# Output projection of a two-layer hybrid trunk: one float32 product becomes three float32r products, with split weights kept in DRAM and one buffer for their high halves

## The chip, the cores and the metric

The kernel runs on one core of a Trainium2 chip. The metric is the device time of one execution in microseconds (us), the median over several executions. The engines are TensorE (PE; its weight loads are shown as PEld), VectorE (DVE), ScalarE (ACT), GpSimd (POOL) and SyncE (SP), which here only issues DMAs.

## The reference

Two layers over x of 1024 rows and 1024 columns, float32. A layer normalises x, multiplies by `w_in` and sends column groups through three mixers (gated DeltaNet with 4 heads, a state space model with 16 heads in 2 groups, retention with 4 heads). Their outputs are normalised, gated and concatenated to `mixed`, 2048 wide. The change is about the last lines:

```python
o_a = rmsnorm(o_a, gdn_norm) * silu(gz)             # 512 columns
o_b = rmsnorm(y_b per group, ssd_norm per group)     # 2 x 512 columns
o_c = rmsnorm(o_c, ret_norm) * silu(rg)             # 512 columns
mixed = concatenate([o_a, o_b, o_c])
out = mixed @ w_out                                 # 2048 x 1024
x = x + rmsnorm(out, post_norm)
```

The weight of each of these norms belongs to a row of `w_out`, so it can be applied to `mixed` or to the rows of `w_out`.

## The kernel before, in words

**Parts.** The work is done in 4 parts: layer 0 rows 0 to 511 (part 0), layer 0 rows 512 to 1023 (part 1), then the same for layer 1 (parts 2, 3). A part of 512 rows is 4 tiles of 128 (`NT`). The float32 product of the input projection is already done as three float32r products: each operand is split in a high part (rounded to float32r) and a low part (the rest), and high x high, low x high and high x low are added. In an even part the weights are split as they arrive (`split`: ACT copies to `w_hi`, POOL subtracts to `w_low`) and both parts are stored to `w_split` in DRAM (`keep`); the odd part after it, of the same layer, loads both from there.

**Input projection.** `w_in` comes in 26 pieces of 256 columns (`PIECES`; two are in SBUF, `W_RING`). A piece is 16 planned `proj` steps, called slices here. The wide pieces use 128x512 matmuls, the narrow ones (gates and retention) 128x256: stationary `hT`, moving `w`, 6 matmuls a slice.

**Output projection.** `mixed` has 4 groups of 512 columns: DeltaNet, two of the state space model, retention. When a group of a part is ready, `mix_turn` transposes its 4 tiles on PE and DVE multiplies each 128x512 bank by the norm weights into `mixT`. Then come its output steps, `("out", p, group, unit, tp)`: the 1024 output columns are 4 units of 256 columns (`UNITS`), and `tp` is a pair of tiles, so 8 steps a group, 32 a part. A unit is 512 KB of `w_out` (128 partitions x 4 row blocks x 256), loaded by SP (line 996) into one of two buffers of `wo_loaded` and used by two steps. A step has 2 x 4 float32 matmuls of 128x256; the trace records each of them as two. DVE adds the bank to `acc` (lines 1572, 1575). After the last unit of group 3 come `squares` and `final` (norm, residual, store).

**Order.** `make_plan` writes out one order of steps for all engines: each engine goes through `plan` and does its share. The planner keeps a clock for each engine, a due time for each result, and picks in this order: side work that is due, a `mix_turn` if no output step is left open, the next mixing step if due within `NEAR` ns, else an output step, if it is due and (the front is late, or stuck, or the next mixing step is more than `OUT_WAIT` away and `APART` slices have gone since the last output step), else the next front step. The front is stuck where `frees` names a buffer still in use: gate pieces 12 and 13 wait for `mix_turn` of group 3 of the part before, 16 and 17 for that of group 0, the retention pieces (from 18 on) for that of group 1, the first piece of the next part for that of group 2. SP's DMAs are one list, `loads`, sorted by the place in the plan that frees their buffer; SP waits for each in turn (line 978: for the stores of `w_split` before a piece buffer is overwritten).

## Time and profile before

| | |
|---|---|
| median of 3 runs | 2396.87 us (2395.07 to 2397.87) |
| the profiled execution | 2396.32 us, its span 2394.5 us |
| granted TensorE clock, mean | 0.996 of full speed |
| busy PE / DVE / ACT / POOL | 2313.7 / 1303.8 / 761.9 / 503.8 us |
| DMA | 339.27 MB, 142 GB/s on the mean |

The span runs from the first to the last instruction. A matmul's duration includes its way through the array, so neighbouring matmuls overlap; the distance between their starts is what one costs. "idle before" is the time an engine stood ahead of an instruction, and behind the arrow is what ended it.

### The profile page before, as it was taken

Reading aid. Unit: us, or ns where it says so; the run is one execution under the profiler, and the core shown is the slowest. Engines: PE = TensorE matmul, PEld = TensorE weight load, DVE = VectorE, ACT = ScalarE, POOL = GpSimd, SP = SyncE. Lnnn points to the kernel's source line nnn. Section 1 sums busy time; section 2 is a strip of 40 time slices with the busy share of each in tenths; the row PEclk is TensorE's granted clock in tenths of the full one; section 3 lists DMA queues with packets and bytes.
Section 4 is the critical chain, followed back from the end, with each engine's and each line's share of the span. In section 5 each row is a group of like instructions: output and inputs, shape, how many; then the busy total and the mean of one; then the engine's idle time right before and its main releaser. Section 6 shows DMA issues by size and latency. Waiting matters only on the chain. (4 is left out here: it accounts for less than half of the span.)

```text
span 2394.5 us, 37085 instructions
## 1 busy us (share of the span) xinstructions
PE 2313.7 (97%) x15032; PEld 2044.7 (85%) x15032; DVE 1303.8 (54%) x2284; ACT 761.9 (32%) x1373; POOL 503.8 (21%) x448
## 2 busy tenths in 40 slices
PE   5999999999999999999999999999999999999995
PEld 4887888998888889899888898889988889889995
DVE  3766578435556565624555756853445554573233
ACT  3644344232423234112444423422233323331000
POOL 2443333330100011101243323423211000110000
PEclk9999999999999999999999999999999999999998
DMA  5644422555323324343544442545632232343412
GB/s 190 230 159 158 159 106 97 190 207 195 122 86 100 116 88 151 131 144 123 203 173 167 167 154 93 184 142 197 237 130 93 93 115 80 129 153 98 158 54 97
DMA packets 78649, 339.27 MB, mean 142 GB/s; under 512 B 8976, under 2 KB 9744, under 8 KB 65040
## 3 DMA queue, kind: packets, MB, share of 16 engines
q1 hardware_dynamic: 77760, 335.45, 41.0%
q8 instruction: 121, 1.98, 0.3%
q10 hardware_dynamic: 720, 1.45, 0.2%
q14 instruction: 48, 0.39, 0.0%
HBM read 219.42 MB, written 117.44 MB: 141 GB/s over the span
## 5 line engine op out<-in xcount | busy, mean ns | idle before, releaser
L1024 PE MATMUL ps<-w_hi,hT_hi 128*128 128x256 f32 x1792 | 526.2, 294 | 1.6 <-POOL w_low L1958 1.6
L1024 PE MATMUL ps<-w_low,hT_hi 128*128 128x256 f32 x1792 | 504.6, 282 | 0.0
L1024 PE MATMUL ps<-w_hi,hT_lo 128*128 128x256 f32 x1792 | 499.8, 279 | 0.0
L1024 PE MATMUL ps<-wo_loaded,mixT 128*128 128x256 f32 x2048 | 457.7, 379 | 3.5 <-DVE et L1592 3.4
L1024 PEld LDWEIGHTS ps<-wo_loaded,mixT 128*128 128x128 f32 x2048 | 384.0, 190 | 60.1 <-issue 5.8
L1958 POOL TENSOR_TENSOR w_low<-w_loaded,w_hi 128x512 fp32r<-128x512 f32 x208 | 284.4, 1384 | 449.1 <-ACT w_hi L1718 449.0
L1024 PEld LDWEIGHTS ps<-wk 128*128 128x128 f32 x2336 | 294.9, 191 | 92.4 <-DVE wk L1479 30.2
L1024 PE MATMUL ps<-wk 128*128 128x128 f32 (+2 forms) x2336 | 343.3, 286 | 11.4 <-DVE wk L1502 1.8
L1024 PEld LDWEIGHTS ps<-w_low,hT_hi 128*128 128x128 f32 x1792 | 340.3, 190 | 1.3 <-issue 0.2
L1024 PEld LDWEIGHTS ps<-w_hi,hT_hi 128*128 128x128 f32 x1792 | 337.0, 188 | 3.8 <-POOL w_low L1958 2.3
L1024 PEld LDWEIGHTS ps<-w_hi,hT_lo 128*128 128x128 f32 x1792 | 339.3, 189 | 0.0
L1024 PE MATMUL ps<-hT_hi,w_hi 128*128 128x512 f32 x768 | 333.9, 435 | 1.1 <-POOL w_low L1958 1.1
L1024 PE MATMUL ps<-hT_lo,w_hi 128*128 128x512 f32 x768 | 303.0, 395 | 0.0
L1024 PE MATMUL ps<-hT_hi,w_low 128*128 128x512 f32 x768 | 301.1, 392 | 0.0
L1387 DVE SCALAR_TENSOR_TENSOR slot<-raw,par,slot 128x512 f32<-128x512 f32 x240 | 215.0, 897 | 48.4 <-ACT slot L1751 32.9
L1575 DVE TENSOR_TENSOR acc<-acc,ps 128x512 f32<-128x512 f32 x96 | 65.8, 686 | 227.7 <-PE ps L1024 227.1
L1024 PEld LDWEIGHTS ps<-hT_lo,w_hi 128*128 128x128 f32 x768 | 144.1, 188 | 35.7
L1024 PEld LDWEIGHTS ps<-hT_hi,w_hi 128*128 128x128 f32 x768 | 145.3, 189 | 22.3 <-POOL w_low L1958 2.7
L1024 PEld LDWEIGHTS ps<-hT_hi,w_low 128*128 128x128 f32 x768 | 145.6, 190 | 20.1
L1718 ACT ACTIVATE w_hi<-w_loaded 128x512 fp32r<-128x512 f32 x208 | 121.2, 621 | 98.4 <-DMA w_loaded<-in_w_in 98.4
L1918 POOL TENSOR_TENSOR rs<-rs,con 128x4 f32<-128x4 f32 x32 | 34.9, 1090 | 477.9 <-DVE rs L1317 477.9
L1489 DVE TENSOR_TENSOR wk<-ps,con 128x512 f32<-128x512 f32 x96 | 66.3, 691 | 101.6 <-PE ps L1024 101.3
(178 smaller groups left out, 2721.1 us busy)
## 6 DMA issues: line engine op xcount, KB each, us to landing
w_loaded<-in_w_in SPq DMA_DIRECT2D x104, 512.0 KB, 5.1
w_split<-w_hi SPq DMA_DIRECT2D x52, 1024.0 KB, 8.1
w_split<-w_low SPq DMA_DIRECT2D x52, 1024.0 KB, 10.1
w_hi<-w_split SPq DMA_DIRECT2D x104, 512.0 KB, 5.5
w_low<-w_split SPq DMA_DIRECT2D x104, 512.0 KB, 6.6
wo_loaded<-in_w_out SPq DMA_DIRECT2D x64, 512.0 KB, 3.6
wk<-in_x SPq DMA_DIRECT2D x8, 512.0 KB, 6.4
xfin<-in_x SPq DMA_DIRECT2D x8, 512.0 KB, 5.2
```

The lines of the kernel that those rows point to most:

```text
L1024: return nc.tensor.matmul(o, a, b, start=start, stop=stop)
L1387: stt(o, r[:, j:j + HALF], w[:, j:j + 1], o, ALU.mult, ALU.add).then_inc(S["conv_done"], 1)
L1489: empty(tt(PP, bank4(s), over_rows(mask), ALU.mult), s)
L1575: empty(tt(o, o, b, ALU.add), s)
L1718: A(w_hi[:, n % W_RING, j * 512:(j + 1) * 512], wr[:, n % W_RING, j * 512:(j + 1) * 512], ACT.Copy)\
L1918: tt(rs[:, 12:16], rs[:, 8:12], pw[:, 0:4], ALU.pow).then_inc(S["o_rstd"], 1)
L1958: tt(w_lo[at], wr[at], w_hi[at], ALU.subtract)\
```

## The change

Each operand of the output projection is split. `mix_turn`: ACT copies the transposed bank to `mixT_hi` (float32r), DVE then subtracts it from the bank into `mixT_lo`; the norm weights go to the units. In an even part a new side step `split_out` takes a raw unit: ACT writes `wo_hi` = unit x norm weight for each row block, DVE writes unit x weight - `wo_hi` into the unit's own buffer (`wo_parts`). SP stores both parts to `wo_split` (`keep_unit`). In an odd part SP loads the low part into the ring of two, as before the unit, and the high part (`high`) into `wo_hi`, of which there is one buffer: it is loaded when the last step of the unit before is done. The four units of the last group of part 3 (`TAIL` and on) are loaded, both parts, into the buffers of the projection pieces after the last projection (`tail`). An output step has 24 float32r matmuls of 128x256 in place of 8 float32 ones. Smaller edits: `rot` lies in `raw`, with a wait of ACT for `ret_sum`; the planner's constants `SPLIT_FROM`, `APART`, `NEAR` and `UNIT` change, and it knows when units are there; the scratch for dynamic DMAs goes from 1024 to 512.

```diff
+            return [("mixT", p, r[0], 2 * r[2] + 1), ("unit", out_no(step))]
+        if k == "split_out":
+            return [("raw", out_no(step))]
...
+                if n == PARTS * len(PIECES) - 1:
+                    for u in range(UNITS):
+                        at["unit", TAIL + u] = dma(MB, "n")
...
+        elif k == "split_out":
+            mark("n", act(1700, *after))
+            mark(("unit", out_no(step)), both(1700, "n"))
         elif k == "out":
             mark("n", pe(UNIT))
+            if r[2] == NT // 2 - 1:
+                u = out_no(step)
+                at["raw", u + 2] = dma(MB // 2, "n")
+                if (u + 1) // (GROUPS * UNITS) % 2 and u + 1 < TAIL:
+                    at["unit", u + 1] = dma(MB // 2, "n")
...
+        if step[0] == "out" and step[4] == NT // 2 - 1:
+            p, u = divmod(out_no(step) + 1, GROUPS * UNITS)
+            if p % 2 == 0 and p < PARTS:
+                sides["unit"].append(("split_out", p, *divmod(u, UNITS)))
...
-        unit = outs[0] if outs and ("small", smalls) in done else None
+        unit = outs[0] if outs and ("small", smalls) in done and (outs[0][1] % 2 or ("split_out", *outs[0][1:4]) in done) else None
...
-SPLIT_FROM = 6
-APART = 20
-NEAR = 150
+SPLIT_FROM = 7
+APART = 10
+NEAR = 300
 FAR = 1e12
-SLICE, LINE, TURN, UNIT, TABLE, MB = 705, 224, 109, 16 * 216, 1283, 3200
+SLICE, LINE, TURN, UNIT, TABLE, MB = 705, 224, 109, 24 * 119, 1283, 3200
+
+
+TAIL = (PARTS * GROUPS - 1) * UNITS
+
+
+def out_no(step):
+
+    return (step[1] * GROUPS + step[2]) * UNITS + step[3]
+
+
+def unit_split_no(u):
+
+    return u - GROUPS * UNITS * ((u // (GROUPS * UNITS) + 1) // 2)
...
+    wo_split = nc.dram_tensor("wo_split", (GROUPS * UNITS, 2, P, 4 * PC), F32, kind="Internal").ap()
...
-        mixT = sb("mixT", 4, HALF)
+        mixT_hi, mixT_lo = sb("mixT_hi", 4, HALF, dtype=F32R), sb("mixT_lo", 4, HALF, dtype=F32R)
+        wo_hi = sb("wo_hi", 4 * PC, dtype=F32R)
...
-        rot = sb("rot", 512)
+        rot = raw[:, 0, 0:512]
...
+            if s[0] == "split_out" or s[0] == "out" and s[1] % 2 and s[4] == 0 and out_no(s) < TAIL:
...
+            if u[0] == "out" and u[1] % 2:
+                loads.append((where[(*out_before(u), NT // 2 - 1)], n, ("high", *u[1:])))
+            elif u[0] == "out":
+                loads.append((where[(*u, 0)], n, ("keep_unit", *u[1:])))
...
+        for u in range(UNITS):
+            loads.append((where["proj", PARTS - 1, len(PIECES) - 1, 1, Q - 1], u, ("tail", PARTS - 1, u)))
...
+                elif kind == "keep_unit":
+                    k = out_no(key)
+                    sp.wait_ge(S["wo_lo_ready"], 4 * unit_split_no(k) + 4)
+                    sp.dma_start(wo_split[k % (GROUPS * UNITS), 0], wo_hi[:].bitcast(F32)).then_inc(wo_hi_kept, 16)
+                    sp.dma_start(wo_split[k % (GROUPS * UNITS), 1], wo_parts[:, n % 2, :].bitcast(F32)).then_inc(wo_kept[n % 2], 16)
+                elif kind == "high":
+                    k = out_no(key)
+                    before = out_before(key)
+                    wait_filled(sp, (*before, NT // 2 - 1))
+                    if before[1] % 2 == 0:
+                        sp.wait_ge(wo_hi_kept, 16 * (unit_split_no(k - 1) + 1))
+                    sp.dma_start(wo_hi[:].bitcast(F32), wo_split[k % (GROUPS * UNITS), 0]).then_inc(wo_hi_in, 16)
+                elif kind == "tail":
+                    for v in range(W_RING):
+                        wait_filled(sp, ("proj", PARTS - 1, len(PIECES) - 1 - v, 1))
+                    k = (GROUPS - 1) * UNITS + n
+                    hi, lo = tail_parts(n)
+                    sp.dma_start(hi.bitcast(F32), wo_split[k, 0]).then_inc(tail_in[n], 16)
+                    sp.dma_start(lo.bitcast(F32), wo_split[k, 1]).then_inc(tail_in[n], 16)
                 else:
                     if n >= 2:
                         wait_filled(sp, unit_use(units[n - 2]))
+                        if kept_units(n - 2):
+                            sp.wait_ge(wo_kept[n % 2], 16 * kept_units(n - 2))
                     if kind == "small":
                         sp.dma_start(wo[:, n % 2, 0:KD * NSM], w_small[p // 2].rearrange("p k n -> p (k n)")).then_inc(wo_in[n % 2], 16)
+                    elif p % 2 == 0:
+                        sp.dma_start(wo[:, n % 2, :], w_out[p // 2, key[2], key[3]]).then_inc(wo_in[n % 2], 16)
                     else:
-                        sp.dma_start(wo[:, n % 2, :], w_out[p // 2, key[2], key[3]]).then_inc(wo_in[n % 2], 16)
+                        k = out_no(key) % (GROUPS * UNITS)
+                        sp.dma_start(wo_parts[:, n % 2, :].bitcast(F32), wo_split[k, 1]).then_inc(wo_in[n % 2], 16)
...
+                    k_out = out_no(s)
+                    if k_out >= TAIL:
+                        hi, lo = tail_parts(u)
+                        if tp == 0:
+                            pe.wait_ge(tail_in[u], 32)
+                    else:
+                        r = unit_no[s[:4]] % 2
+                        hi, lo = wo_hi[:], wo_parts[:, r, :]
+                        if tp == 0 and p % 2:
+                            loaded_unit(pe, s[:4])
+                            pe.wait_ge(wo_hi_in, 16 * (k_out - GROUPS * UNITS * (p // 2 + 1) + 1))
+                    hi, lo = (a.rearrange("p (k n) -> p k n", k=4) for a in (hi, lo))
                     b = opened(s)
-                    if tp == 0:
-                        loaded_unit(pe, s[:4])
                     for v in range(2):
                         t = 2 * tp + v
                         wait_emptied(pe, ("mix_turn", p, G, t))
+                        o = b[:, v * PC:(v + 1) * PC]
                         for kk in range(4):
-                            i = mm(b[:, v * PC:(v + 1) * PC], mixT[:, kk, t * P:(t + 1) * P], w[:, kk, :], kk == 0, kk == 3)
+                            if p % 2 == 0 and tp == 0 and v == 0:
+                                pe.wait_ge(S["wo_lo_ready"], 4 * unit_split_no(k_out) + kk + 1)
+                            m_hi, m_lo = (m[:, kk, t * P:(t + 1) * P] for m in (mixT_hi, mixT_lo))
+                            mm(o, m_hi, hi[:, kk, :], kk == 0, False)
+                            mm(o, m_hi, lo[:, kk, :], False, False)
+                            i = mm(o, m_lo, hi[:, kk, :], False, kk == 3)
...
-                        empty(tt(mixT[:, :, t * P:(t + 1) * P], bank4(tag), over_cols(par[:, l, Q_MIX + 4 * s[2]:Q_MIX + 4 * s[2] + 4]),
-                                 ALU.mult), tag)
+                        dve.wait_ge(S["mix_hi"], NT * (GROUPS * p + s[2]) + t + 1)
+                        empty(tt(mixT_lo[:, :, t * P:(t + 1) * P], bank4(tag), mixT_hi[:, :, t * P:(t + 1) * P], ALU.subtract), tag)
+                elif k == "split_out":
+                    r = unit_no["out", *s[1:]] % 2
+                    for kk in range(4):
+                        dve.wait_ge(S["wo_hi_ready"], 4 * unit_split_no(out_no(s)) + kk + 1)
+                        at = slice(kk * PC, (kk + 1) * PC)
+                        q = Q_MIX + 4 * s[2] + kk
+                        stt(wo_parts[:, r, at], wo[:, r, at], par[:, l, q:q + 1], wo_hi[:, at], ALU.mult, ALU.subtract)\
+                            .then_inc(S["wo_lo_ready"], 1)
...
+                elif k == "mix_turn":
+                    for t in range(NT):
+                        tag = (*s, t)
+                        wait_filled(act, tag)
+                        A(mixT_hi[:, :, t * P:(t + 1) * P], bank4(tag), ACT.Copy).then_inc(S["mix_hi"], 1)
+                elif k == "split_out":
+                    u = ("out", *s[1:])
+                    k_out = out_no(s)
+                    r = unit_no[u] % 2
+                    loaded_unit(act, u)
+                    if k_out:
+                        before = out_before(u)
+                        wait_filled(act, (*before, NT // 2 - 1))
+                        if before[1] % 2 == 0:
+                            act.wait_ge(wo_hi_kept, 16 * (unit_split_no(k_out - 1) + 1))
+                    for kk in range(4):
+                        at = slice(kk * PC, (kk + 1) * PC)
+                        q = Q_MIX + 4 * s[2] + kk
+                        A(wo_hi[:, at], wo[:, r, at], ACT.Copy, scale=par[:, l, q:q + 1]).then_inc(S["wo_hi_ready"], 1)
...
+                        if m == 0 and p:
+                            act.wait_ge(S["ret_sum"], 2 * RH * p)
```

## Rows read from the trace of the kernel before

**Rows 1.** The page: busy us, share and count of engines; one group of instructions.

```profile
PE 2313.7 (97%) x15032; PEld 2044.7 (85%) x15032; DVE 1303.8 (54%) x2284; ACT 761.9 (32%) x1373; POOL 503.8 (21%) x448
...
L1024 PE MATMUL ps<-wo_loaded,mixT 128*128 128x256 f32 x2048 | 457.7, 379 | 3.5 <-DVE et L1592 3.4
```

**Rows 2.** Stretches: length, busy us and count of PE, PEld, DVE, ACT, POOL, clock, DMA, GB/s.

```profile
0.00:345.00 345.00, 305.82 (x1885) 259.27 (x1886) 202.85 (x352) 151.55 (x289) 122.08 (x103) 1.00 0.48 173
345.00:2300.00 1955.00, 1937.56 (x12789) 1722.99 (x12788) 1069.09 (x1887) 603.31 (x1072) 375.73 (x336) 1.00 0.41 139
2300.00:2370.00 70.00, 70.00 (x362) 62.42 (x360) 21.51 (x36) 4.74 (x9) 1.75 (x3) 1.00 0.22 68
2370.00:2394.50 24.50, 0.31 (x2) 0.00 (x0) 10.37 (x9) 2.33 (x5) 4.19 (x6) 0.58 0.43 150
```

**Rows 3.** PE in order of time, two narrow pieces: start us, us, what.

```profile
1019.78 0.28 PE L1024 MATMUL ps<-w_hi,hT_hi 128*128 128x256 f32 x1
...
1023.88 0.28 PE L1024 MATMUL ps<-w_hi,hT_lo 128*128 128x256 f32 x1
...
2296.08 0.28 PE L1024 MATMUL ps<-w_hi,hT_hi 128*128 128x256 f32 x1
...
2299.92 0.28 PE L1024 MATMUL ps<-w_hi,hT_lo 128*128 128x256 f32 x1
```

**Rows 4.** PE in order of time: output steps of parts 1 and 2.

```profile
976.80 7.17 PE L1024 MATMUL ps<-wo_loaded,mixT 128*128 128x256 f32 x32 [0.67 <-DVE et L1592]
...
987.43 3.62 PE L1024 MATMUL ps<-wo_loaded,mixT 128*128 128x256 f32 x16
...
994.39 13.98 PE L1024 MATMUL ps<-wo_loaded,mixT 128*128 128x256 f32 x64
...
1477.07 10.52 PE L1024 MATMUL ps<-wo_loaded,mixT 128*128 128x256 f32 x48
...
1497.46 7.17 PE L1024 MATMUL ps<-wo_loaded,mixT 128*128 128x256 f32 x32 [0.67 <-DVE et L1592]
...
2082.33 17.48 PE L1024 MATMUL ps<-wo_loaded,mixT 128*128 128x256 f32 x80
```

**Rows 5.** PE in order of time, from the last projection on.

```profile
2300.04 1.03 PE L1027 MATMUL ps<-con,slot 128*128 128x128 f32 x8
2300.91 3.62 PE L1024 MATMUL ps<-wo_loaded,mixT 128*128 128x256 f32 x16
...
2314.58 0.38 PE L1024 MATMUL ps<-st_r,wk 128*128 128x128 f32 x2
2314.80 0.61 PE L1024 MATMUL ps<-slot,wk 128*128 128x128 f32 x4
2315.25 3.62 PE L1024 MATMUL ps<-wo_loaded,mixT 128*128 128x256 f32 x16
...
2323.50 17.43 PE L1024 MATMUL ps<-wo_loaded,mixT 128*128 128x256 f32 x80
...
2342.51 27.79 PE L1024 MATMUL ps<-wo_loaded,mixT 128*128 128x256 f32 x128
```

**Rows 6.** Loads of a unit, line 996: time from issue to landing.

```profile
DMA to landing us min/median/max: 3.3/3.6/13.4
```

**Rows 7.** DMA in the 18 us from 582 to 600, where a piece is loaded.

```profile
DMA packets 720, 2.62 MB, mean 146 GB/s; under 512 B 80, under 2 KB 80, under 8 KB 720
...
q1 hardware_dynamic: 720, 2.62, 43.8%
```

**Rows 8.** Single lines: count, ns min/median/max, first and last start, shapes.

```profile
L1798 ACT ACTIVATE wk<-ps,dec x56: 345/368/369, 136.7 to 1997.6; 128x128 f32<-128x128 f32 x56
...
L1751 ACT ACTIVATE slot<-raw,par x48: 721/724/729, 60.1 to 1902.5; 128x512 f32<-128x512 f32 x48
...
L1744 ACT ACTIVATE raw<-ps x96: 576/583/594, 59.5 to 2082.6; 128x512 f32<-128x512 f32 x96
...
L1343 DVE SCALAR_TENSOR_TENSOR hT_lo<-ps,par,hT_hi x128: 340/343/352, 23.0 to 1738.6; 128x128 fp32r<-128x128 f32 x128
...
L1387 DVE SCALAR_TENSOR_TENSOR slot<-raw,par,slot x240: 734/750/1897, 64.1 to 2106.9; 128x512 f32<-128x512 f32 x120
...
L1958 POOL TENSOR_TENSOR w_low<-w_loaded,w_hi x208: 1261/1289/2262, 18.6 to 1703.6; 128x512 fp32r<-128x512 f32 x104
```

**Rows 9.** SP's own waits: us in total, times, longest.

```profile
SPq L978 <- DMA w_split<-w_low: 404.5, 48, 11.7
```

More of the change, by code:

```diff
@@ L500, in make_plan @@
     done, smalls = {("small", -1)}, -1
-    sides = {k: [] for k in ("ssd", "fin", "norm", "post", "scale", "split")}
+    sides = {k: [] for k in ("ssd", "fin", "norm", "post", "scale", "split", "unit")}
+    sides["unit"].append(("split_out", 0, 0, 0))
     turns = [("mix_turn", p, g) for p in range(PARTS) for g in range(GROUPS)]
@@ L887, in hybrid_kernel @@
                 units.append(("small", s[1]))
-            if s[0] == "out" and s[4] == 0:
-                units.append(s[:4])
+            if s[0] == "split_out" or s[0] == "out" and s[1] % 2 and s[4] == 0 and out_no(s) < TAIL:
+                units.append(("out", *s[1:4]))
         unit_no = {u: i for i, u in enumerate(units)}
+        out_before = lambda u: ("out", (out_no(u) - 1) // (GROUPS * UNITS), *divmod((out_no(u) - 1) % (GROUPS * UNITS), UNITS))
         unit_use = lambda u: u if u[0] == "small" else (*u, NT // 2 - 1)
@@ L942, in x_rows, with tail_parts, kept_units @@
             return (x if p < 2 else x1)[r:r + P, :]
+        def tail_parts(u):
+            at = (slice(None), u // 2, slice(u % 2 * 4 * PC, (u % 2 + 1) * 4 * PC))
+            return w_hi[at], w_lo[at]
+        def kept_units(n):
+            return sum(units[m][0] == "out" and units[m][1] % 2 == 0 for m in range(n % 2, n + 1, 2))
         @block.sync
@@ L1417, in _ @@
                         wait_emptied(dve, tag)
-                        tt(own, own, rot[:], ALU.add).then_inc(S["ret_sum"], 1)
+                        tt(own, own, rot, ALU.add).then_inc(S["ret_sum"], 1)
                         dve.wait_ge(S["ret_sum"], m + 1)
```

16 lines of the change are left out of this document (10 added, 6 removed).

## Prediction

> **What bounds the kernel now.** I read the table of engines first: TensorE (PE) is busy for 2313.7 of 2394.5 us, VectorE (DVE) for 1303.8, ScalarE (ACT) for 761.9 [rows 1]. Then the stretches: of PE's 80.8 us without work, 39.2 lie in the first 345 us, 17.4 in the 1955 us up to 2300, none from 2300 to 2370, and 24.2 in the rest, behind the last matmul [rows 2]. So what PE issues is the time; every us of PE work removed counts, unless a new wait takes its place. The other engines matter only as sources of such waits. The third view is PE's order of time, in which one sees how long an output step takes and which steps stand directly behind one another.
>
> **The matmuls.** There are 128 output steps (4 parts, 4 groups, 4 units, 2 pairs of tiles). The 2048 matmul records [rows 1] are 16 to a step, two for each float32 matmul. A run of 128 records takes 27.79 us with a tail of about 0.16 on the last one, so 216 ns each and 3.46 us a step [rows 5]. The new step has 24 float32r matmuls of 256 columns. The narrow projection pieces already issue this form: 36 of them start between 1019.78 and 1023.88, 117 ns apart, and 33 between 2296.08 and 2299.92, 120 ns apart [rows 3]. Weight loads are in those pitches. A step then costs 24 x 117 = 2.81 to 24 x 120 = 2.88 us. The saving is 128 x 0.65 = 83 at one end and 128 x 0.58 = 74 at the other; I take **78 us**.
>
> **One high buffer in the odd parts.** In parts 1 and 3 the high half of unit u+1 may only be loaded when PE has done unit u. SP then issues it (0.33 us) and a 512 KB load lands 3.3 to 13.4 us after issue, median 3.6 [rows 6]. With the hand-over I put a reload at 3.9 us (3.6 to 13.7). It is free when PE has a mixing step or projection slices to do in between, and exposed when units follow one another. In the order of before they do at these places: part 1 group 0 has three boundaries between units, in the stretch from 976.80 to the end of the run at 994.39; part 3 group 0 has the same three 1164 us later, part 1 group 3 has three from 1477.07 on [rows 4], part 3 groups 1 to 2 four behind the last projection [rows 5]. Between these steps PE does nothing, or 0.7 to 3.5 us of other work. Taking off that work, the 13 boundaries lack 8.2 + 8.2 + 8.2 + 12.5 = 37 us. That is the upper end if the order stays; the lower is 0, if the changed planner fills all of them. It knows the load time of a unit now, asks for 10 instead of 20 projection slices between units, and of before's 128 steps 110 lie ahead of 2300 (all but the 18 of [rows 5]), one in 18 us on the mean of the 1955 us [rows 2], so there is room for more of them ahead of the places where the front is stuck, and the bunches shrink. For the three bunches outside the end (24.6 us) I take half, 12 us.
>
> The end is worse than its four boundaries. The last projection matmul is at 2299.92 [rows 3]; behind it came 18 output steps: two of group 1, eight of group 2 (the last five in one run), eight of group 3 [rows 5]. With the closer spacing about 12 remain: two units of group 2 and the four of group 3. At the same moment SP issues the tail, 8 x 512 KB, into the buffers of the projection pieces, and the next high reload stands behind it on the same queue. 2.62 MB took a 43.8% share of 18 us, so 332 GB/s while it ran [rows 7]; 4.19 MB take 12.6 us and the reload lands some 15 us after the last projection. PE has meanwhile one unit (5.7 us) and the steps of the last retention head (0.9 for each of two steps and four of about 0.7, from the starts in [rows 5]), 10 us. I take 4 us for that and 4 for one more reload: 8, bounds 0 and 16. Group 3 itself has both halves resident and waits for nothing once they landed. In all the odd parts cost **20 us** (0 to 41).
>
> Worked from a page: the Trainium skill, "DMA: Bandwidth & Descriptors", in the section on the anatomy of one DMA, puts a DMA at a fixed 2.0 us plus its bytes at 436 GB/s, an estimate of 3.2 us for 512 KB and 11.6 us for the tail's 4.19 MB. By it the odd parts would cost about 3 us less. It was fitted to another DMA path; the rows are of this one, and the sum uses them.
>
> **Splitting in the even parts.** Parts 0 and 2 load 32 raw units; ACT writes the scaled high half in four pieces of 128x256 and DVE subtracts. No such piece is in the trace. ACT's scaled copy takes 368 ns for 128 columns and 724 for 512, DVE's scalar_tensor_tensor 343 and 750 [rows 8]; at 256 I take 0.49 and 0.48. Bounds are those neighbours. PE needs both halves of row block kk before its three products with it, and neither can start before the previous unit is done (one high buffer). The last block is ready 4 x 0.49 + 0.48 = 2.4 us after, PE would have reached it in 1.1, so an exposed boundary costs 1.4 us when both engines are free, 3.9 when the halves follow one another. Units directly behind one another in the even parts are at six boundaries (two in the run of 80 records at the end of part 2 [rows 4] and two in the like run of part 0, two in group 0 of part 2). With half of them left, **4 to 12; I take 6**; if all six stay, up to 23.
>
> **Work on ACT and DVE.** The norm multiplication on DVE (64 times) becomes a subtraction of the same shape, so 0; ACT gets 64 copies of 583 ns from PSUM and 128 pieces of 0.49, 100 us; DVE gets 128 x 0.48 = 61 us [rows 8]. At 37% and 58% of the new span this is covered by slack, but not each wait: the DVE subtraction now waits for ACT, and what is queued behind it on DVE (conv taps, bank emptying) waits too; ACT waits in split_out for the store of the previous high half before it may overwrite it, with the silus, conv starts and weight splits of the next piece behind it. That store sits in SP's queue, and SP stands 404.5 us in the two even parts waiting for w_split stores, up to 11.7 us at a time [rows 9]. A unit has at least 5.7 us, mostly with 10 projection slices of 0.7 us (six matmuls at 117 ns) between, so most are covered. NEAR rises from 150 to 300, which lets PE stand up to 0.3 us before a mixing step. For all of this I take **6 us**, 0 to 20. The moved `rot` and the 32 x 2 stores of 512 KB I put at nothing: DMA engines are at 22 to 48% in the stretches [rows 2]. Without that cover a delayed piece load would stop PE by what its landing exceeds the 11 us of a piece.
>
> GpSimd's subtraction for w_low took 1289 ns at the median but up to 2262 [rows 8]. The Trainium skill, "SBUF — State Buffer", in the section "SBUF: two separate sides", says that a DVE operation with two SBUF inputs locks out a GpSimd operation that reads SBUF; the new DVE pieces are of that kind. It speaks against the change: a w_low piece could come up to 0.48 us later each time. PE stood still for all reasons together for 17.4 us in 1955, so a delay of that size is inside the 0 to 20 above.
>
> **Sum.** -78 + 20 + 6 + 6 = -46 us. The profiled execution took 2396.3 us (span 2394.5 and 1.8 around it), so 2350; the median of the runs is 0.6 higher, so **2351 us**. The steps after the last matmul are as before.
>
> **Rivals.**
> *Everything is hidden* (chance 0.10): the planner dissolves the bunches and only 5 to 15 us come back: 2324 to 2334. For it speaks that PE stood still for only 17.4 us in 1955; against it that the front is stuck before pieces 16 and 18 until whole groups are out, and that the tail's loads stand before a reload.
> *The reloads keep their bunches* (0.14): 37 for the boundaries of the odd parts and 8 for the tail's loads, 12 to 15 even, 6 to 10 on ACT: -78 + 63 to 70, 2382 to 2389; with a few filled from 2372.
> *Slower* (0.08): reloads land late. The 28 reloads of the odd parts share SP's queue with the piece loads (2 MB each). If each exposed 2.8 us or more, 28 x 2.8 = 78 and the saving is gone; at the longest landing seen, 13.4 us, they would add far more. Median landing near 7 us in all of the bunches and no interleaving would do it: 2400 to 2420. Against it: median 3.6, and projections can be put between.
> *No change that can be told* (0.04): the same between 2392 and 2401. This measurement tells about 0.2%, 5 us.
> The forecast's case, 2334 to 2372, has 0.64.
>
> **Range.** 2326 to 2386 leaves out a fifth of each of the first two rivals (0.05), all of the third and of no change (0.12), and some for the edges of the cases themselves: about 0.2. Faster by over 0.2% is 0.64 + 0.10 + 0.14 = 0.88.
>
> **What would show it.** Output matmuls 117 to 120 ns apart, PE's busy time down by some 75; PE idle up by 25 to 40, of it 5 to 12 between the last projection and the last output step, waiting for DMA on wo_hi, and waits on DVE wo_parts in the bunches of even parts; ACT busy near 862 and DVE near 1365. Landing of wo_hi near 4 us. The prediction is wrong if the idle time stays near 81 (first rival), if wo_hi is awaited at most of the 28 boundaries, or if ACT stands for the high store and the projections stop with it.

## The result, and the profile after

The changed kernel takes **2384.03 us** (median of 4 runs, 2379.87 to 2384.77) against 2396.25 before: ratio **0.9945, 95% interval 0.9928 to 0.9962**, 12 us faster where 45 were forecast. The profiled execution took 2384.77 us, its span is 2383.0. First the page of the changed kernel: the engines, and one group of the new matmuls.

```profile
PE 2267.2 (95%) x16056; PEld 2043.6 (86%) x16056; DVE 1355.3 (57%) x2412; ACT 849.4 (36%) x1567; POOL 510.5 (21%) x448
...
L1101 PE MATMUL ps<-wo_hi,mixT_hi 128*128 128x256 f32 x960 | 276.2, 288 | 5.1 <-issue 3.8
```

PE's busy time fell by 46.5 us, and its time without work rose from 80.8 to 115.8 us. The same four stretches as in [rows 2], cut where the order now puts them, of the changed kernel:

```profile
0.00:345.00 345.00, 300.81 (x1844) 255.37 (x1845) 204.90 (x353) 149.22 (x282) 120.14 (x100) 0.99 0.44 161
345.00:2290.00 1945.00, 1902.79 (x13701) 1725.85 (x13700) 1119.97 (x2018) 690.36 (x1266) 384.40 (x339) 1.00 0.47 167
2290.00:2359.00 69.00, 63.58 (x515) 62.43 (x513) 20.31 (x36) 7.43 (x15) 1.75 (x3) 0.98 0.22 86
2359.00:2383.00 24.00, 0.00 (x0) 0.00 (x0) 10.16 (x9) 2.35 (x5) 4.22 (x6) 0.54 0.43 154
```

PE lacked work for 44.2, 42.2, 5.4 and 24.0 us in them, against 39.2, 17.4, 0 and 24.2. So most of the loss lies in the long middle, spread out. The busy column hides more of it: a matmul at half clock counts as busy, and so does a pause that is shorter than the tail of the matmul before it (they last 0.28 us at 0.12 us from start to start). I therefore took the distance between neighbouring starts of all matmuls, and split what exceeds the pitch of that form: single pauses over 0.15 us, and the excess in the stretches whose granted clock was half. The starts shift at one place, and this comes first. Where a float32r matmul follows a plain float32 one, its start is shown only 28 ns behind the last float32 record, and the start after it comes later by what is missing. PE of the kernel before, an output step and the projection behind it:

```profile
1024.00 3.61 PE L1024 MATMUL ps<-wo_loaded,mixT 128*128 128x256 f32 x16
1027.26 0.47 PE L1024 MATMUL ps<-w_hi,hT_hi 128*128 128x256 f32 x1
1027.57 0.28 PE L1024 MATMUL ps<-w_low,hT_hi 128*128 128x256 f32 x1
```

The 16 records take 3.26 us up to the start of the first projection matmul, and the second follows after 0.31 us, not 0.12. Together that is 16 x 216 ns and one pitch of 0.12. It is so at all 54 places where a projection follows an output step, so what is late in the second start belongs to the float32 matmul, and the table counts it there. From the first to the last matmul (computed from the start times in both traces, us):

| | before | after | |
|---|---|---|---|
| output matmuls, without pauses | 442.4 | 364.8 | -77.6 |
| pauses ahead of mixing steps | 60.4 | 100.6 | +40.2 |
| pauses ahead of output steps | 4.5 | 6.0 | +1.5 |
| pauses ahead of projections | 3.7 | 8.1 | +4.4 |
| excess at half clock | 0 | 8.5 | +8.5 |
| mixing and projection matmuls, without pauses | 1838.0 | 1849.1 | +11.1 |
| first to last matmul | 2348.9 | 2337.1 | -11.8 |

By size, all pauses of 0.3 to 0.6 us rose from 17 (7.4 us) to 111 (45.8 us), those over 1 us from 4 (12.5) to 14 (32.3). These counts, and those of the experiments, are made without that correction; with it they are 16 and 101 for the short ones. PE's waits, first of before, then of the changed kernel, show the same (us in total, times, longest):

```profile
...
PE ps L1024 <- DVE et L1592: 3.4, 5, 0.7
PE ps L1024 <- POOL w_low L1958: 2.7, 5, 0.7
...
PE ps L1024 <- issue: 1.1, 4, 0.3
```

```profile
...
PE ps L1101 <- issue: 13.4, 37, 3.8
PE ps L1101 <- DVE wk L1415: 6.8, 8, 1.6
PE ps L1101 <- DVE st_g L1604: 5.6, 26, 0.2
...
PE ps L1104 <- ACT dec L1846: 5.5, 2, 2.9
```

Waits on "issue" rose from 4 to 37: one is that for the reload of `wo_hi` (3.8 us), the 36 others are 0.27 us long, ahead of mixing matmuls. "issue" says that the profile names nothing that ended them. One of them in order of time, DVE, then PE, shows that the operand had only just come:

```profile
138.82 0.35 DVE L1589 SCALAR_TENSOR_TENSOR wk<-ps,dec,wk 128x128 f32<-128x128 f32 x1 [0.58 <-PE ps L1101]
...
139.24 0.30 PEld L1101 LDWEIGHTS ps<-wk 128*128 128x128 f32 x2 [0.43 <-issue]
139.27 0.46 PE L1101 MATMUL ps<-wk 128*128 128x128 f32 x2 [0.27 <-issue]
```

DVE's operation into `wk` ends at 139.17, the weight load that reads `wk` starts at 139.24: the step was issued ahead of its operand. Between 137.2 and 142.5 the kernel before has a projection slice between any two mixing steps.

**One long pause, followed back.** In order of time around 631 us of the changed kernel: ACT, then SP, then PE.

```profile
631.51 1.71 ACT L1838 ACTIVATE wo_hi<-wo_loaded,par 128x256 fp32r<-128x256 f32 x4 [8.77 <-DMA wo_loaded<-in_w_out]
...
639.87 0.37 ACT L1846 ACTIVATE dec<-ps 128x240 f32<-128x240 f32 x1
...
628.33 0.33 SPq L1070 DMA_DIRECT2D wo_loaded<-in_w_out  x1
...
640.30 0.84 PE L1104 MATMUL ps<-con,cum 128*128 128x128 f32 x4 [2.61 <-ACT dec L1846]
```

ACT stands 8.8 us in `split_out` for the raw unit. SP issued that load at 628.33, right behind the last matmul of the unit before (started at 628.02): `split_small` had taken a place in the ring of two, so the load needed that unit's buffer. The planner dates every load two units ahead and does not know it. ACT's `dec` then comes late and PE waits for `gdn_decay`; the same stands at 1787. Behind the pause the granted clock is half (the number behind the engines' times: 0.58 of full on the mean of this window, against 1.00 further on):

```profile
640.00:644.00 4.00, 3.70 (x19) 3.71 (x20) 1.12 (x2) 3.92 (x7) 0.00 (x0) 0.58 0.82 333
700.00:704.00 4.00, 3.51 (x29) 3.16 (x27) 2.00 (x6) 0.37 (x1) 0.00 (x0) 1.00 1.03 407
```

The trace has six such stretches of 3.4 us (from 81, 286, 364, 641, 1791 and 2327), each at a pause of 1.7 to 3.9 us. At 642 the output matmuls start 213 ns apart, at 644 again 118: the 1.2 GHz level against the 2.4 GHz one.

### The profile page after: what moved, and what is told of

Read it like the earlier page. It is cut to its first block and busy times, and to the rows that moved or that the text cites. A ratio compares the mean times of both kernels' runs of the same rounds, so it can differ in the third digit from the quotient of the medians.

```text
span 2383.0 us, 39741 instructions
## 1 busy us (share of the span) xinstructions
PE 2267.2 (95%) x16056; PEld 2043.6 (86%) x16056; DVE 1355.3 (57%) x2412; ACT 849.4 (36%) x1567; POOL 510.5 (21%) x448
## 5 line engine op out<-in xcount | busy, mean ns | idle before, releaser
L2079 POOL TENSOR_TENSOR w_low<-w_loaded,w_hi 128x512 fp32r<-128x512 f32 x208 | 287.5, 1398 | 418.2 <-ACT w_hi L1818 418.1
L1101 PE MATMUL ps<-hT_hi,w_hi 128*128 128x512 f32 x768 | 326.3, 425 | 3.9 <-POOL w_low L2079 3.8
L1101 PE MATMUL ps<-wo_hi,mixT_hi 128*128 128x256 f32 x960 | 276.2, 288 | 5.1 <-issue 3.8
L1101 PE MATMUL ps<-wo_hi,mixT_lo 128*128 128x256 f32 x960 | 272.5, 284 | 0.0
L1101 PE MATMUL ps<-wo_parts,mixT_hi 128*128 128x256 f32 x960 | 272.0, 283 | 0.0
L1101 PEld LDWEIGHTS ps<-wo_hi,mixT_hi 128*128 128x128 f32 x960 | 183.8, 191 | 7.8 <-issue 5.1
L1101 PEld LDWEIGHTS ps<-wo_parts,mixT_hi 128*128 128x128 f32 x960 | 183.1, 191 | 2.1 <-issue 1.2
L1101 PEld LDWEIGHTS ps<-wo_hi,mixT_lo 128*128 128x128 f32 x960 | 183.3, 191 | 0.0
```

What stands on the lines that cost most here:

```text
L1101: return nc.tensor.matmul(o, a, b, start=start, stop=stop)
L2079: tt(w_lo[at], wr[at], w_hi[at], ALU.subtract)\
```

## The experiments

Times are medians; ratios are against the kernel before on the same chip. "Pauses" are those defined above; "half clock" is the length of those stretches.

**The planner's constants in the changed kernel.**

*near150*:

```diff
-NEAR = 300
+NEAR = 150
```

> The changed kernel with the planner's NEAR back at 150 ns, nothing else. Theory N: the 39 us that TensorE stands more in pauses of 0.3 to 0.6 us (112 of them, 17 before) come from NEAR = 300, which lets it go to a mixing step 0.3 us before its operands are due instead of doing one more slice. Then these pauses fall to about 20 and the time to 2350 to 2362 us. Rival S: the mixing steps are late because ScalarE and VectorE do and wait more (ScalarE stands 125 us ahead of its wo_hi copies); then the pauses stay above 80 and the time is 2378 to 2388.

Measured: 2399.71 us, ratio 1.0005 (0.9995 to 1.0014). Pauses of 0.3 to 0.6 us fell from 45.8 to between 11 and 16 us (by how those inside the stretches of half clock are counted) as expected, but those over 1 us rose from 32.3 to 55.2, those of 0.6 to 1 from 8.7 to 20.9, and half clock from 20.5 to 68.3 us. The short pauses were exchanged for long ones at a loss of 16 us.

*step_near150*:

```diff
-        if step and due(step) <= now + NEAR:
+        if step and due(step) <= now + 150:
```

> The changed kernel with 150 ns for the next mixing step alone; the output steps and the transposes ahead of them keep 300. Theory N: as good as NEAR = 150 throughout, 2350 to 2362 us, within 5 us of it. If it stays within 5 us of the changed kernel (2384) while NEAR = 150 throughout is faster, it is the output steps that are sent too early. Rival S: both stay at 2378 to 2388.

Measured: 2402.3 us, ratio 1.0015 (0.9989 to 1.0041), half clock 81.9 us, pauses over 1 us 55.6. As the one before: the place where NEAR acts is the choice of the next mixing step, not that of the output step.

*apart20*:

```diff
-APART = 10
+APART = 20
```

> The changed kernel with APART back at 20, so output steps are spread less and stand in bunches before pieces 16 and 18 and at the end, as before. Theory B (the spread order is what hides the reloads of the one high buffer): waits for wo_hi and for the split halves rise from about 10 us to 30 to 45, time 2400 to 2420. Rival: the reloads are hidden whatever the order, or the narrower spacing itself costs as much as it gives: 2375 to 2390.

Measured: 2504.35 us, ratio 1.0449 (1.0431 to 1.0467), far slower than either theory had it. PE waited for a reload of `wo_hi` nine times, 25.5 us in all, and for the halves of a split 13.4 us, together the 30 to 45 us expected:

```profile
PE ps L1101 <- DVE wo_parts L1661: 13.4, 6, 4.1
```

(The 19 pauses and 45.5 us of a later expectation are these fifteen and four that end with DVE's `et`.) But half clock rose to 116 us and the pauses ahead of mixing steps to 146 us, and these were in neither theory. With units asked for only every 20 slices, many stay over for the places where the front is stuck, and there the single high buffer is exposed.

**The same constants in the kernel before.**

*before_near300*:

```diff
-NEAR = 150
+NEAR = 300
```

> The kernel before with NEAR at 300, nothing of the split products. Theory N: the same pauses of 0.3 to 0.6 us appear without the change, 80 to 120 of them, time 2420 to 2432 us (+25 to +35). Rival S: NEAR does next to nothing by itself, 2393 to 2401.

Measured: 2435.08 us, ratio **1.016 (1.0145 to 1.0175)**, 38 us slower. Pauses of 0.3 to 0.6 us: 96 (39.4 us), against 17 (7.4), half clock 10.2 us. Its list of PE's waits has the same entry, grown from 4 times:

```profile
PE ps L1024 <- issue: 10.2, 38, 0.3
```

So the value of 300 makes those pauses, without any of the change's splitting.

*before_apart10*:

```diff
-APART = 20
+APART = 10
```

> The kernel before with APART = 10 alone. Theory: where a unit needs no reload and no split, it does not matter where the output steps stand, 2392 to 2402 us. Rival: spread steps leave too few to fill the pauses of the state space groups and the end, 2405 to 2425, and part of the changed kernel's loss is APART's.

Measured: 2402.16 us, ratio 1.0019 (1.0009 to 1.0028): 4 us, small but clear of the noise, here where units need no high buffer.

**The store of the high half.** In *act_store* ACT issues it itself, behind its four copies:

```diff
-                    sp.dma_start(wo_split[k % (GROUPS * UNITS), 0], wo_hi[:].bitcast(F32)).then_inc(wo_hi_kept, 16)
+                    act.wait_ge(S["wo_hi_ready"], 4 * unit_split_no(k_out) + 4)
+                    act.dma_start(wo_split[k_out % (GROUPS * UNITS), 0], wo_hi[:].bitcast(F32)).then_inc(wo_hi_kept, 16)
```

> The changed kernel; the store of a split unit's high half is issued by ScalarE's own DMA queue right behind the four copies, no longer by SP behind its waits for the w_split stores. Same order of steps. Theory S (ScalarE standing for the high store makes small2 and other mixing steps late): ScalarE's standing ahead of wo_hi falls from 125 us to under 70, the two pauses of 2.8 and 3.1 us behind dec go, and the 3.4 us at half clock after each; time 2370 to 2379 us. Rival: ScalarE has slack enough and stands for the unit before in any case: 2381 to 2387, no change.

Measured: 2387.44 us, ratio 0.9956 (0.9941 to 0.9971). ACT stands ahead of wo_hi for 124.5 us in place of 125.4. In *plan_store* the planner is told to wait for the store:

```diff
-            return [("raw", out_no(step))]
+            return [("raw", out_no(step)), ("kept", out_no(step) - 1)]
...
+            mark(("kept", out_no(step)), dma(MB // 2, ("unit", out_no(step))) + 5000)
```

> The changed kernel; the planner is told that a unit may only be split once the high half of the one before is stored (its DMA time plus 5 us), so split_out stands later in ScalarE's order. Theory S: ScalarE no longer stands in front of other work, the long pauses go, 2368 to 2380 us. Rival: the later splits hold back the output steps, which then fall into the bunches: 2390 to 2430.

Measured: 2383.38 us, ratio 0.9936 (0.9921 to 0.9951). Both as the changed kernel: with NEAR 300 the store is not what ACT stands for.

*near225*, the changed kernel with NEAR = 225, ran beside them:

> The changed kernel with NEAR = 225, between 150 (2400) and 300 (2384). Theory O (the order is a matter of luck: what NEAR saves in short pauses, 30 us, an order that nobody checked gives back in pauses over 1 us and the half clock behind them): the time follows the number of pauses over 1 us and not NEAR, anywhere from 2360 to 2400; short pauses of 0.3 to 0.6 us between 40 and 112. Rival N: time and pauses move steadily with NEAR; then 2388 to 2396.

Measured: 2406.67 us, ratio 1.0031 (1.002 to 1.0043): short pauses 11.0 us, over 1 us 63.5, half clock 68.3. The time does not go from 2400 to 2384 steadily with NEAR, it goes with the long pauses.

**The date of the raw load.** In *raw_true* the planner's view is set right, nothing else:

```diff
         elif k == "split_small":
+            clock["small_from"] = clock.get("begun_unit")
...
         elif k == "split_out":
+            clock["begun_unit"] = out_no(step)
...
+                if clock.get("small_from") == u:
+                    clock["small_from"] = None
+                    at["raw", u + 1] = dma(MB // 2, "n")
                 at["raw", u + 2] = dma(MB // 2, "n")
```

> The planner is told what the ring of two really does: the raw load of the unit that comes after the small weights starts only when the unit before is done (in the changed kernel the planner dates it one unit earlier, while at 631.5 us ACT waited 8.8 us for that load and PE then paused 2.8 us before gdn_decay, the same 3.1 us at 1787, each followed by 3.4 us at half clock). Nothing else is changed. Theory R (long pauses come from dates that the planner has wrong, and the half clock behind them doubles their price): the two pauses and the two stretches at half clock behind them are gone, ACT stands ahead of the wo_hi copies for some 105 in place of 125 us, and the time is 2384 - (2.8 + 3.1) - 2 x 1.7 = 2375, 2372 to 2379. Rival L (any new order brings its own long pauses somewhere, as the versions with another NEAR did): other pauses over 1.7 us appear, 2381 to 2395.

Measured: **2375.51 us** (2373.48 to 2377.66), ratio 0.9905 (0.9892 to 0.9918). Both pauses before `gdn_decay` and the half clock behind them are gone; ACT stands 107.6 us. Two more stretches of half clock (near 286 and 364) are gone though the pauses there stayed (1.9 and 1.7 us), one is new near 1570, and that at the end is 6.8 us long, so not all of the 8.5 us need be the date's. The window that holds the place:

```profile
636.00:642.00 6.00, 6.00 (x39) 5.37 (x38) 4.32 (x7) 4.43 (x5) 1.43 (x1) 1.00 0.66 264
```

**One or two high buffers.** Room for a second one is in the residual rows' buffer; the control, *no_residual*, leaves out their loads only, and its last addition takes the post weights in place of those rows.

```diff
-                    sp.dma_start(xfin[:], x_rows(p, key[2])).then_inc(xf_in, 16)
+                    pass
...
-                    dve.wait_ge(xf_in, 16 * (n + 1))
-                    tt(acc[:, t, :], acc[:, t, :], xfin[:], ALU.add)
+                    tt(acc[:, t, :], acc[:, t, :], post[:], ALU.add)
```

> Leaves out the loads of the residual rows x (final adds the post weights in their place, so the last addition is of other data of the same shape and place); it is the control for the two-high-buffer version, whose buffer takes the 4 KB of those rows. 16 loads of 512 KB fewer, the plan is the same. Expected within 3 us of the changed kernel, 2381 to 2387, pauses at the same places. Rival: the residual loads stand in SP's queue before others, and without them pauses shrink: 2370 to 2380.

Measured: 2372.81 us, ratio 0.99 (0.9885 to 0.9914). The pauses are the same ones; all of the 11 us lie behind the last matmul (14.0 in place of 24.5 us), where three residual loads followed one another through one buffer.

*two_high* (the core of the edit; PE, ACT, DVE and SP take the buffer by the unit's parity):

```diff
-        wo_hi = sb("wo_hi", 4 * PC, dtype=F32R)
+        wo_hi2 = sb("wo_hi", 2, 4 * PC, dtype=F32R)
...
-                if (u + 1) // (GROUPS * UNITS) % 2 and u + 1 < TAIL:
-                    at["unit", u + 1] = dma(MB // 2, "n")
+                if (u + 2) // (GROUPS * UNITS) % 2 and u + 2 < TAIL:
+                    at["unit", u + 2] = dma(MB // 2, "n")
```

> As the control without residual loads, but with two high buffers by the unit's parity in their 4 KB, and the planner told of it: a split or reload of the next unit may run while PE uses the one before. Theory of the prediction (the single high buffer costs 20 us in odd parts and 6 in the even ones): 2384 - 26 = 2358, 2350 to 2366. Theory D, from the trace of the changed kernel (wo_hi awaited 5.6 us in 3 pauses, split halves 5.7 in 43 small ones): 2384 - 11 = 2373, 2368 to 2378, the 3.9 us pause behind the last projection gone and the half clock behind it too. Theory O (the buffer is hidden by the order, and what costs is the order's own short pauses): 2380 to 2390, with as many pauses of 0.3 to 0.6 us as before, about 112.

Measured: 2409.93 us, ratio 1.0043 (1.0029 to 1.0056), 37 us slower than its control. Pauses ahead of output steps fell to 6.4 us from 8.0, those ahead of mixing steps rose from 100.5 to 123.5; the two before `gdn_decay` are now 5.7 and 6.8 us, half clock 51 us. None of the three expectations was met.

*two_high_apart20* is the same with APART = 20:

> The two-high-buffer version with 20 projection slices asked for between units in place of 10. With one high buffer that change cost 120 us (2504), wo_hi was awaited for 45.5 us in 19 pauses and half clock held for 116 us. If the single buffer in bunches is the cause of that, two buffers bring it back to within 20 us of the version with 10 slices: 2375 to 2405, wo_hi awaited under 15 us. If the bunches themselves (front stuck, other buffers) are the cause, it stays at 2450 to 2500.

Measured: 2398.46 us, ratio 1.0002 (0.9994 to 1.0011). With one buffer the same constant gave 2504; about 10 us of the difference are the missing residual loads, the rest, over 90, is what one high buffer costs when units stand in bunches. Of it 30 us are waits for the buffer itself: for reloads 25.5 us there and 0.2 here, for halves of a split 13.4 and 8.7. The others are half clock (116 and 37 us long) and longer pauses ahead of mixing steps.

*two_high_raw* is two_high with the edit of raw_true:

> Two high buffers in the place of the residual rows (those loads left out, the last addition is of the post weights), and the planner told the true date of the unit load behind the small weights. Without that date two buffers took 2409.9, against 2372.8 of the control with one: the pauses before gdn_decay, waiting for ACT's dec, were 5.7 and 6.8 us in place of 2.8 and 3.1, half clock 51 in place of 20.5 us. Theory D (two buffers let splits stand earlier in ACT's queue, where the late unit load holds up more): these pauses are gone and the time is 2409.9 - 12.5 - 8 = 2390 or less; with the rest of the difference also from it, down to 2363. Rival (two buffers cost by something else): 2400 to 2412.

Measured: 2382.85 us, ratio 0.9944 (0.9931 to 0.9956), 27 us less than with the false date: the long pauses before `gdn_decay` are gone, half clock is 24 us. The false date made most of the loss. ACT's waits ahead of wo_hi fell to 14 us (30 in two_high, 108 in raw_true), so it was the buffer held by PE that ACT stood for; nobody waited for ACT there. Still it is 10 us above the control with one buffer and the false date: the second buffer buys nothing here, where PE stood for the one buffer only once, 3.9 us (see below).

**NEAR 150 again, with true dates.**

*true_near150* has the edits of raw_true, plan_store and near150:

> The planner knows both late dates (the unit load behind the small weights, and the store of the high half before the next split: 5 us behind its issue), and NEAR is 150 as before the change. With NEAR 150 alone the short pauses of 0.3 to 0.6 us fell from 46 to 16 us, but pauses over 1 us rose to 55 us and half clock to 68 us, time 2400; its 7 us pause lay behind a split whose ACT part waited for the store of the high half, two of 2.8 behind the unit load. Theory D (wrong dates made the long pauses): they go, the short ones stay at 16 us, and from 2375.5 (raw_true) the 30 us come back: 2345 to 2358. Rival C (with NEAR 150 the order is so tight that some other engine is late somewhere): pauses over 1 us stay above 40 us, 2375 to 2400.

Measured: 2397.19 us, ratio 1.0001 (0.9992 to 1.001).

*raw_true_near150* has those of raw_true and near150:

> As the one before, but the planner does not know the store of the high half. Theory D: it keeps a pause of some 7 us behind a split in the first part, and with the half clock behind it stands 8 to 20 us above the version that knows both dates, 2355 to 2375. Rival C: no different from that version within 5 us.

Measured: 2392.52 us, ratio 0.9985 (0.9976 to 0.9994). The theory of the dates fails for NEAR 150: pauses over 1 us stay at 52 and 49 us, half clock at 72 in both. The longest that an edit could reach, in the order of time of the version with both dates, SP, ACT, DVE:

```profile
404.78 0.81 SPq L1041 DMA_DIRECT2D w_loaded<-in_w_in  x2
405.63 0.43 SPq L1052 DMA_DIRECT2D wo_split<-wo_hi  x1
...
412.53 1.71 ACT L1844 ACTIVATE wo_hi<-wo_loaded,par 128x256 fp32r<-128x256 f32 x4 [2.90 <-DMA wo_split<-wo_hi]
...
413.07 1.68 DVE L1667 SCALAR_TENSOR_TENSOR wo_parts<-wo_loaded,par,wo_hi 128x256 fp32r<-128x256 f32 x4 [5.59 <-ACT wo_hi L1844]
```

The high half was split from 394.8 on, its store waited in SP's list behind a piece load until 405.6, ACT stood for it, DVE behind ACT, and PE 6.5 us behind DVE (at 417.5). *raw_act_near150* has the edits of act_store, raw_true and near150:

> NEAR 150, the true date of the unit load, and the store of the high half issued by ACT right behind the split, in place of SP. In both versions with NEAR 150 and this date (2392.5 and 2397.2) the longest pause, 6.4 to 6.5 us near 412, hangs on this store: the split ended at about 397, but SP issued the store only at 405.6, behind a piece load that it stood for, and it landed at 412.5. Theory Q (SP's list is what holds the store up): issued by ACT it lands near 404.5, that pause and the half clock behind it go, 2392.5 - 6.4 - 1.7 = 2384, down to 2375 if other splits gain too. Rival C (the tight order moves the pause elsewhere): within 4 us of 2392.5. With NEAR 300 the same edit changed nothing (2387.4 against 2384.0).

Measured: 2389.94 us, ratio 0.9969 (0.9957 to 0.9981). That pause fell from 6.4 to 3.9 us (ACT now comes to the split late for other work), half clock from 72 to 55 us. Expected were 2384 or less; the intervals of the two versions still overlap. The other long pauses stayed.

**Towards a better kernel.** In *raw_rest* the last three residual rows go to `hT_lo`, free after the last projection, on top of the true raw date:

```diff
+                elif kind == "rest" and p == PARTS - 1 and key[2]:
+                    wait_filled(sp, ("proj", p, len(PIECES) - 1, 1))
+                    sp.dma_start(last_rows(key[2]), x_rows(p, key[2])).then_inc(xf_last[key[2]], 16)
```

> The version with the true date of the unit load, and the residual rows of the last three tiles of part 3 loaded behind the tail into hT_lo, which is free after the last projection, in place of one after the other into xfin. The control without residual loads ended 10.5 us sooner behind the last matmul (14.0 in place of 24.5 us), with the same pauses ahead of it. Expected: 2375.5 - 10.5 = 2365, 2361 to 2369, 14 us behind the last matmul. Rival: the loads behind the tail delay the reload of the high half or the last units, and a few us come back: 2369 to 2376.

Measured: 2369.88 us, ratio 0.9881 (0.9866 to 0.9897). Behind the last matmul 14.0 us, as expected, but the rival took 4 to 5 of it back: the reload of wo_hi behind them was awaited 6.9 us. *raw_rest_tail* puts the tail behind that reload, and the residual rows behind the first output step of the last group:

```diff
-            loads.append((where["proj", PARTS - 1, len(PIECES) - 1, 1, Q - 1], u, ("tail", PARTS - 1, u)))
+            loads.append((where["out", PARTS - 1, GROUPS - 2, UNITS - 1, 0], u, ("tail", PARTS - 1, u)))
```

> raw_rest with the tail's 8 loads placed in SP's list behind the last reload of the high half, and the three residual loads behind the first output step of the last group. In raw_rest the reload behind the last projection was awaited 6.9 us (2.9 in raw_true), the half clock after it 3.4 us or more. Expected: that reload lands 3.3 to 4 us after its issue, the pause is under 1 us, and the time 2369.9 - 6 - 2 = 2362, 2358 to 2365. Rival: the tail's first unit is now late for the last group (1 MB behind the reload, 5.7 us for it), 2365 to 2372.

Measured: **2359.59 us** (2357.39 to 2361.95), ratio **0.9839 (0.9825 to 0.9852)**, 38 us below the kernel before and 24 below the changed one. SP issues the last reload first, then the eight tail loads; the page's engines, then SP in order of time, of this version.

```profile
PE 2260.0 (96%) x16056; PEld 2036.8 (86%) x16056; DVE 1355.5 (58%) x2412; ACT 849.5 (36%) x1567; POOL 512.6 (22%) x448
```

```profile
2307.15 0.32 SPq L1066 DMA_DIRECT2D wo_hi<-wo_split  x1
2307.57 0.38 SPq L1072 DMA_DIRECT2D w_hi<-wo_split  x1
...
2312.52 1.43 SPq L1020 DMA_DIRECT2D hT_lo<-x_mid  x3
```

No pause over 1 us is left ahead of an output step, and one stretch of half clock (3.4 us) in the whole kernel.

## Why the prediction failed

The time lies in the forecast range and in that of the second rival (2382 to 2389), but not by that rival's mechanism: the reloads did not keep their bunches.

**The matmuls (-78; measured -78).** This term was right, on both sides: 442.4 us for 128 steps before is 3.46 us a step, as read from the run of [rows 5], and 364.8 us after is 2.85 us, forecast 2.81 to 2.88 (with the pauses under 0.15 us in it).

**One high buffer (+20; measured 6).** The reload itself was forecast well:

```profile
L1054 SPq DMA_DIRECT2D wo_hi<-wo_split x28: 319/320/327, 838.9 to 2317.9; - x28
...
DMA to landing us min/median/max: 3.1/3.4/8.2
```

PE waited for a landing once, for the reload issued at 2317.9 behind the tail, which took 8.2 us:

```profile
2326.21 0.36 PE L1101 MATMUL ps<-wo_hi,mixT_hi 128*128 128x256 f32 x1 [3.75 <-issue]
```

That is 3.9 us from start to start and 1.7 for the half clock, where 8 stood. At the other 27 reloads no pause of PE ends with the landing, where 12 stood. (The expectations count 3 pauses, 5.6 us; the two others, 0.8 us at 422 and 1567, end with DVE's `et`, as such pauses did before [rows 4].) The bunches were dissolved, and apart20 shows what does it: with 20 slices between units the same reloads cost 14 us outside the end. The step on the tail's loads was right in mechanism; putting them behind the reload, and the residual loads behind both, gave 10 us against raw_rest. The estimate from the Trainium skill ("DMA: Bandwidth & Descriptors", "Anatomy of one DMA"), 3.2 us for 512 KB, lies 0.2 below the measured median and would have changed nothing.

**Splitting in the even parts (+6; no wait shown).** PE's list of waits has no entry for `wo_parts` in the changed kernel. The 43 small pauses of 5.7 us in the expectation of two_high are not waits: 14 are matmuls at half clock, the other 29 are the second start behind a float32 matmul, late as at 1027.57 above. So two high buffers had little to win. The pieces took 497 ns on ACT and 480 on DVE, forecast 0.49 and 0.48.

**Work and waits on ACT and DVE, with NEAR (+6, bounds 0 to 20; measured about +60: this is the step that failed).** With 77.6 gained on the matmuls and 5.6 lost on the buffer, 60 us are left over: pauses ahead of mixing steps 40.2, half clock 6.8, small excess of the mixing and projection matmuls 11.1, the pauses ahead of projections and of other output steps 2.0. I had read the edit of NEAR, wrote that it "lets PE stand up to 0.3 us before a mixing step", and did not multiply. It applies at every mixing step that waits for another engine: 84 more of them paused for 0.3 to 0.6 us, 34 us together. before_near300 shows this price alone, 78 more such pauses and 31.5 us. The second part are the pauses over 1 us, 20 us more (3.9 of them the reload), with the half clock behind them. Two of them (5.9 us and 3.4 of half clock) come from a date that the planner has wrong; raw_true, without them, is 8.5 us faster. That ACT would stand for the high store, as I feared, is seen only in the versions with NEAR 150; with 300 it does not matter.

The multiplication would have repaired the number and not the step. With NEAR at 150 the short pauses go and the term is larger, about 74 us by the same count: in near150 pauses ahead of mixing steps are 35 us above those of the kernel before, those ahead of projections 9 us, and the excess at half clock is 27 us. So the waits behind the added work were priced at about a tenth under either constant. No run leaves that work out, and none has SPLIT_FROM or the place of `rot` alone: how much each has in it stays open.

**Could the short pauses be had back?** Not by NEAR: 150 and 225 gave more in long pauses and half clock. What makes these is only partly settled: the raw load's date and SP's list account for some 5 to 7 and 3 us of it. Several pauses stood through near150 and the three versions built on it, among them 5.7 us ahead of a `mix_turn`, 2.5 to 2.9 for w_low and 4.0 for `wk`, and were not followed further. Whether the planner's order at 150 can be kept from them stays open.

**The signs.** Of those named, PE's idle time came as forecast (+35, forecast 25 to 40), but by luck: it was to be made of waits for wo_hi and wo_parts, and is made of pauses ahead of mixing steps. None of the three signs of being wrong came, and none was named for the term that failed. PE's busy time did not come so (-46.5, forecast -75), though the matmuls gained what was forecast: half clock and pauses under the tail of a matmul count as busy. DVE's busy time was forecast at 1365 and came to 1355, ACT's 862 and 849. GpSimd's w_low subtraction took 1292 ns at the median and 2347 at most, against 1289 and 2262 [rows 8], mean 1398 against 1384: the lock-out that the Trainium skill describes ("SBUF — State Buffer", "SBUF: two separate sides") would show here, and these 14 ns a piece, 208 times, are 3 us of POOL's time in all, which is not the bound.

## What to carry to other kernels

Multiply a tolerance in a scheduler by the number of places where it applies before calling it small: 150 ns more gave 84 more pauses and 34 us here. Then run it at the old value too: here the short pauses went, longer ones came, and nothing was won. A list scheduler is as good as its dates; where an engine stands many us for a load, compare the plan's date for that load with the trace, and order a queue by when things are needed, not by when their buffer is free. Read pauses and granted clock together: busy time counts half-clock work as work, and a matmul at half clock, or one that is shown late behind a float32 matmul, looks like a short wait. Call a pause a wait for a buffer only where the buffer's event ends it.

## What the runs showed of the hardware

The granted clock fell to half for 3.4 us at pauses that were mostly shorter than that: in the changed kernel at six pauses of 1.7 to 3.9 us. But not by a rule on the pause alone: the pause of 1.6 us ahead of the same matmuls near 361 us was followed by half clock in the changed kernel and not in the last version, and one of 1.2 us near 1566 was followed by it in raw_true and in the last version, but not in the changed kernel. A float32 matmul of 128x256 is shown as two records, 216 ns apart in a run. Behind the last of them a float32r matmul is shown 28 ns later and the one after that 305 ns later (35 places with 128x256 behind it, pitch 118), so the sum is as if each had its own pitch, and nothing is saved at the change of form. PE at the pause of 1.6 us, in the changed kernel (half clock behind it) and in the last version (none):

```profile
...
362.62 1.55 PE L1101 MATMUL ps<-et,wk 128*128 128x64 f32 x12 [1.58 <-DVE wk L1415]
```

```profile
...
360.72 2.91 PE L1113 MATMUL ps<-et,wk 128*128 128x64 f32 x18 [1.57 <-DVE wk L1427]
```
